# One stretch of filler products per inverse level instead of two, in a two-block transformer kernel

## The chip, the cores and the metric

The kernel runs on one core of one Trainium2 chip. The metric is the device time of one execution in microseconds, the median of several runs. TensorE does the matrix products, VectorE (DVE) and ScalarE (ACT) the elementwise work and the copies out of PSUM, GpSimd (POOL) a little elementwise work, and SyncE (SP) issues the weight transfers.

## The reference, cut to what matters

Two blocks run one after the other on a sequence of 256 tokens of width 1024, all in float32. The first has a mixer and a mixture-of-experts layer, twice. The second is this, for each of two layers, cut to the branch that the change touches:

```python
def rwkv7_scan(r, w, k, v, kk, a):
    # S_t = S_{t-1} diag(w_t) - (S_{t-1} kk_t) (kk_t * a_t)^T + v_t k_t^T ; y_t = S_t r_t
    ...

def rwkv_branch(r, k, v, wl, al, gate, w0, w_up, a0, a_up, k_k, k_a, r_k, lnx_g, lnx_b):
    ...
    y = rwkv7_scan(r_h, w_h, k_h, v_h, kk, a_h)
    mu = jnp.mean(y, axis=-1, keepdims=True)
    var = jnp.mean(jnp.square(y - mu), axis=-1, keepdims=True)
    y = ((y - mu) * lax.rsqrt(var + GN_EPS)).reshape(B, S, W_C) * lnx_g.astype(f32) + lnx_b.astype(f32)
    bonus = jnp.sum(r_h * k_h * r_k.astype(f32), axis=-1, keepdims=True) * v_h
    out = (y + bonus.reshape(B, S, W_C)) * jax.nn.silu(gate.astype(f32))
```

Around it stand the input projection `h @ w_in` (its columns hold the queries, keys and values of three branches, their gates, and three merge gates of width 1024), two attention branches, and the merge of the three.

## The kernel before, in words

**The recurrence.** The kernel does not step through the 256 tokens. It cuts them into chunks of 64 and turns each chunk into small matrices. A layer `l` has 8 heads, in two halves `p` of 4, so `recurrence(l, p)` runs four times. Its heart is the inverse of 16 triangular 64x64 matrices, by doubling: it starts from 2x2 blocks and takes five levels (`for n in range(1, LEVELS)`). A level is a closed chain of three engines:

- TensorE, `step` (L1749): 16 products of 64x64, for two head groups `hh`. Before it TensorE waits for VectorE's updates of the level before (`Sv.at("inv", *K, n - 1, hh)`) and for a mask by GpSimd (`level`).
- ScalarE (L978): one copy out of PSUM per `hh`, signal `step`.
- TensorE: `transposed` (L1762) and `forward` (L1755), 32 products of 64x64 in all (24 in the last level), each group waiting for its copy.
- VectorE (L2591): one subtraction per `hh`, signal `inv`, which starts the next level.

**The filler.** While TensorE waits for such links it takes products from a generator, `fill_tiles(l)` (L1641). Each `next(filler)` issues one dense product of 128x128 by 128x256, called a unit here. A layer has 12 jobs of 16 units (the gates of the three branches, then six tiles of merge gates), 192 units, and the assertions below `filled_by` want all 192 used by the end of `recurrence(l, 1)`. How many units stand at which point is written out by hand in `FILLS`: in "level" before the change, one between `step` and the wait for its first copy, and two behind the products, ahead of the next level. Jobs alternate between PSUM banks 7 and 6; job `n` may start when ScalarE has taken job `n - 2` out (`fill_out`). ScalarE does that at the points where `filled(point)` finds, from `FILLS`, that a job is complete. The weights of the jobs pass through a ring of four slots, and every second job's last product frees one (`used`), for which SyncE waits before it issues the next transfer.

**The norm.** Behind the recurrence's reads, TensorE makes the mean (`gn_mean`, L1892), VectorE centres (L2621), ScalarE squares (L996), TensorE sums (`gn_sum`, L1896), ScalarE makes the inverse root (L1000, L1002), and VectorE scales, adds and multiplies (L2517 to L2517), signal `o`. `fill("gn_mean")` stands between the two TensorE products, `fill("gn_sum")` behind the second. With `p` = 1 two projections of the next stage (`latent`, L1260) stand between `gn_sum` and its filler. With `p` = 0 the next `recurrence(l, 1)` follows the filler, beginning with the `lora` products (L1688); ScalarE's first work there (L949) waits for `o`.

Of the kernel before, what the change touches and what calls it, by code (L numbers as in the profile page):

```python
# [52 lines left out]
H2 = 8  # L53
FILL_POINTS = ["open", "down", "lora", "kk_sum", "rk_sum", "tok"] + ["level"] * (LEVELS - 1) + [
    "w1", "gh", "y0", "move1", "move2", "read", "gn_mean", "gn_sum"]
FILL = dict(tok=6, level=3, w1=2, gh=2, y0=2, move1=1, move2=1, read=2, gn_mean=4)
FILLS = {(0, 0): dict(FILL, open=6, down=0, lora=5, kk_sum=15, rk_sum=8, gn_sum=27),
         (1, 0): dict(FILL, open=4, down=2, lora=11, kk_sum=14, rk_sum=8, gn_sum=22),
         (0, 1): dict(FILL, open=0, down=0, lora=6, kk_sum=15, rk_sum=8, gn_sum=32)}
FILLS[1, 1] = FILLS[0, 1]  # L60
BRANCHES = (2, 0, 1)
NORM_FILL = (0, 6, 6, 10, 4, 6, 8, 8, 16, 16, 16)
# [263 lines left out]
def two_block_program(nc, w, out, cum_rows, marks, order):  # L326
# [34 lines left out]
    with ExitStack() as ctx:  # L361
# [18 lines left out]
        def bank(b, n=HALF):  # L380
            return ps_t[:, b * HALF:b * HALF + n]
# [259 lines left out]
        def filled_by(l, p, point):  # L641

            before = sum(FILLS[l, 0][x] for x in FILL_POINTS) if p else 0
            return (before + sum(FILLS[l, p][x] for x in FILL_POINTS[:point + 1])) // (2 * KD)

        for l in range(2):
            assert filled_by(l, 1, len(FILL_POINTS) - 1) == 12
            assert sum(FILLS[l, p][x] for p in range(2) for x in FILL_POINTS) == 12 * 2 * KD
        POINTS = len(NORM_FILL)
# [524 lines left out]
        def _(pe):  # L1174
# [82 lines left out]
            def project(dst, lhs, rhs, n=KD):  # L1257

                for k in range(n):
                    mm = M(dst, lhs(k), rhs(k), start=k == 0, stop=k == n - 1)  # L1260
                return mm
# [319 lines left out]
            def second(l):  # L1581
# [29 lines left out]
                filler = fill_tiles(l)  # L1611
                for _ in range(FILLS[l, 0]["open"]):
                    next(filler)
                if l:
# [4 lines left out]
                    project(bank(2, T)[0:32], lambda k: vdw[:, k], lambda k: s2["rkv"][:, 2, k], 4).then_inc(*Sp.up("v_down"))  # L1619
                    for _ in range(FILLS[l, 0]["down"]):  # L1620
                        next(filler)
# [5 lines left out]
                for p in range(2):  # L1627
                    recurrence(l, p, lora, ht, filler)
                attention_parts(l)

            def fill_tiles(l):

                for n, (key, i, _) in enumerate(fill_jobs(l)):
                    if i == 0:
                        pe.wait_ge(*has_landed(key))
                    if n >= 2:
                        pe.wait_ge(*S("fill_act").at(l, n - 2))
                    for x in range(2):
                        for k in range(KD):
                            c = (2 * i + x) * P  # L1640
                            mm = M(bank(fill_bank(n))[:, x * T:x * T + T], slot(key)[:, k, c:c + P], s2["ht"][:, k],  # L1641
                                   start=k == 0, stop=k == KD - 1)
                            if x and k == KD - 1:
                                if i:
                                    mm.then_inc(used, 1)
                                else:
                                    mm.then_inc(*S("fill_pe").up(l, n))
                            yield
# [24 lines left out]
            def recurrence(l, p, lora, ht, filler):  # L1673
                Sa, Sp, Sv, So = S("rwkv_act"), S("rwkv_pe"), S("rwkv_dve"), S("rwkv_pool")
                K = (l, p)
# [41 lines left out]
                for r, (jj, tt) in enumerate(pairs):  # L1717
                    for hh, half, o in ((0, 0, 0), (1, 1, 0), (1, 0, T)):
                        for c in range(2):
                            rows, tok = halves[hh], slice(tt * P + 64 * c, tt * P + 64 * c + 64)  # L1720
# [20 lines left out]
                inv, prod, wk, gh = rw["inv"], rw["prod"], rw["wk"], rw["gh"]  # L1741
# [4 lines left out]
                def step(n, hh, r, c):  # L1746

                    rows = halves[c]
                    return M(bank(2 + hh)[halves[(c + hh) % 2], r * 64:r * 64 + 64], rw[f"lev{n % 2}"][rows, r, hh], inv[rows, hh, 0, r],  # L1749
                             start=True, stop=True)  # L1750

                def forward(hh, r, c):

                    rows = halves[c]
                    return M(bank(hh)[halves[(c + hh) % 2], r * 64:r * 64 + 64], inv[rows, hh, 1, r], prod[rows, hh, r],  # L1755
                             start=True, stop=True)

                def transposed(hh, r, c):

                    rows = halves[c]  # L1760
                    o = (256, 3 * HALF)[hh] + r * 64
                    return M(ps_t[rows, hh * HALF + o:hh * HALF + o + 64], prod[rows, hh, r], inv[rows, hh, 1, r],  # L1762
                             start=True, stop=True)

                each = [(r, c) for r in range(4) for c in range(2)]
                for n in range(1, LEVELS):
                    pe.wait_ge(*So.at("level", *K, n))
                    for hh in range(2):
                        pe.wait_ge(*Sv.at("inv", *K, n - 1, hh))
                    for r in range(4):  # L1770
                        for hh in range(2):
                            for c in range(2):
                                mm = step(n, hh, r, c)
                            if r == 3:
                                mm.then_inc(*Sp.up("step", *K, n, hh))
                    next(filler)
                    if n == 1:
                        pe.wait_ge(*Sv.at("gk", *K))
                    pe.wait_ge(*Sa.at("step", *K, n, 0))
                    for r, c in each:  # L1780
                        mm = transposed(0, r, c)
                    pe.wait_ge(*Sa.at("step", *K, n, 1))
                    if n == LEVELS - 1:
                        mm.then_inc(*Sp.up("inv", *K, n, 0))
                        for r, c in each:
                            mm = forward(1, r, c)
                        mm.then_inc(*Sp.up("inv", *K, n, 1))
                    else:
                        for r in range(4):
                            for hh in range(2):  # L1790
                                for c in range(2):
                                    mm = forward(hh, r, c)
                                if (r, hh) == (3, 0):
                                    mm.then_inc(*Sp.up("inv", *K, n, 0))
                        for r, c in each:
                            mm = transposed(1, r, c)
                        mm.then_inc(*Sp.up("inv", *K, n, 1))
                    for _ in range(FILLS[K]["level"] - 1):
                        next(filler)

                vt, bht, kht = rw["v_tok"], rw["bh_tok"], rw["kh_tok"]
# [1202 lines left out]
```

## Time and profile before

| | |
|---|---|
| median of 3 runs | 2031.74 us (2028.92 to 2032.73) |
| profiled execution | 2032.98 us, its span 2031.2 us |
| TensorE busy | 1653.0 us, 81% of the span |
| VectorE, ScalarE, GpSimd busy | 27%, 16%, 5% |
| mean granted TensorE clock | 0.909 |

The span is cut into 40 slices of 50.8 us. The first 24 are the first block, which reads the experts' weights; the second block begins near 1222 us. In the rows below, PE is TensorE's products and PEld its weight loads. Every float32 product shows as two records of each, so a unit is two PE records, and `x4` is two units. The time behind `[` is how long the engine had been idle before the row, and behind `<-` stands what ended it. The end of a PE record is modelled and overlaps the next one, so lengths of TensorE work are best taken from start to start. A row of a stretch (A:B) has its length, then for PE, PEld, DVE, ACT and POOL the busy time with the number of records (for one line alone, PE and PEld only), then the mean granted clock (1.00 is 2.4 GHz, 0.50 is 1.2 GHz), the DMA share and GB/s. A row of waits has the total, the number of waits and the longest; `issue` means that nothing in the profile ended it.

### The profile page before, as it was taken

How to read it: one execution, taken by the hardware profiler on the slowest of the kernel's cores; microseconds unless marked ns; L12 is line 12 of the kernel's file. 1: busy time of each engine (PE TensorE's matmuls, PEld its weight loads, DVE VectorE, ACT ScalarE, POOL GpSimd, SP SyncE). 2: the span in 40 equal slices, each digit the busy share in tenths (PEclk: the TensorE clock that was granted, in tenths of full speed). 3: DMA queues.
4: the chain of work that ended last, by engine and by line, in shares of the span. 5: the costliest groups of instructions: out<-in, count | busy, mean ns of one | idle time of the engine just before them, and what ended most of it. 6: DMA issues, size and time to landing. Idle time of an engine off the chain costs nothing.

```text
span 2031.2 us, 25724 instructions
## 1 busy us (share of the span) xinstructions
PE 1653.0 (81%) x11442; PEld 946.6 (47%) x11442; DVE 543.5 (27%) x1029; ACT 335.0 (16%) x723; POOL 106.4 (5%) x129
## 2 busy tenths in 40 slices
PE   6988765666757997565656569999999999999999
PEld 3544221111215862111212118777578687775785
DVE  0455010000105652000101012553343225533432
ACT  1131100000000001000000001343332013423320
POOL 0000000000000001000000000210020002100200
PEclk8998898877888998787888779999999999999999
DMA  9988999999999969999999992321443331214330
GB/s 403 385 372 341 426 428 428 428 428 428 428 428 425 393 264 415 423 428 427 428 428 428 428 426 94 126 85 48 187 145 125 135 144 65 92 48 172 146 125 21
DMA packets 45740, 588.66 MB, mean 290 GB/s; under 512 B 5184, under 2 KB 5344, under 8 KB 9920
## 3 DMA queue, kind: packets, MB, share of 16 engines
q1 hardware_dynamic: 42624, 575.05, 68.7%
q0 software_dynamic: 2576, 10.54, 1.3%
q8 instruction: 90, 1.47, 0.3%
q10 hardware_dynamic: 432, 1.44, 0.2%
q14 instruction: 18, 0.15, 0.0%
HBM read 585.96 MB, written 1.06 MB: 289 GB/s over the span
## 4 chain that ended last, share of the span: by engine, by line
PE 56%; DMA 38%; DVE 3%; ACT 2%; issue 1%; SPq 0%; ACTq 0%; DVEq 0%
DMA arena<-in_experts 37%; PE ps L1260 17%; PE ps L1641 8%; PE ps L1528 5%; PE ps L1664 4%; PE ps L1660 4%; PE ps L1433 3%; PE ps L2015 3%; DMA ring<-in_stream 1%; PE ps L1762 1%; PE ps L2028 1%; PE ps L1749 1%; PE ps L2071 1%; PE ps L1224 1%; PE ps L1540 1%
## 5 line engine op out<-in xcount | busy, mean ns | idle before, releaser
L1528 PE MATMUL ps<-arena 128*32 128x512 f32 x1532 | 246.3, 768 | 149.3 <-DMA arena<-in_experts 144.7
L1528 PE MATMUL ps<-ring,arena 128*32 128x512 f32 x1488 | 232.6, 755 | 148.5 <-DMA ring<-in_experts 148.3
L1528 PEld LDWEIGHTS ps<-arena 128*32 128x32 f32 x1532 | 49.8, 126 | 303.0 <-DMA arena<-in_experts 150.4
L1528 PEld LDWEIGHTS ps<-ring,arena 128*32 128x32 f32 x1488 | 47.0, 124 | 304.1 <-DMA ring<-in_experts 180.6
L1641 PE MATMUL ps<-arena,ring 128*128 128x256 f32 x768 | 188.0, 388 | 0.0
L1260 PE MATMUL ps<-arena,ring 128*128 128x256 f32 (+1 forms) x960 | 184.1, 354 | 2.5 <-ACT arena L754 2.5
L1260 PEld LDWEIGHTS ps<-arena,ring 128*128 128x128 f32 x960 | 163.6, 193 | 22.7 <-ACT arena L754 3.1
L1641 PEld LDWEIGHTS ps<-arena,ring 128*128 128x128 f32 x768 | 139.8, 190 | 29.4 <-issue 10.1
L2448 DVE TENSOR_TENSOR arena<-ps,gate 128x512 f32<-128x512 f32 x16 | 10.3, 686 | 315.6 <-PE ps L1528 315.6
L1660 PE MATMUL ps<-arena,ring 128*128 128x256 f32 x384 | 89.5, 382 | 0.0
L862 ACT ACTIVATE arena<-ps,modcol 128x128 f32<-128x128 f32 x32 | 14.6, 457 | 439.0 <-PE ps L1540 439.0
L1664 PE MATMUL ps<-ring,arena 128*128 128x512 f32 x192 | 85.7, 592 | 0.0
L1260 PE MATMUL ps<-arena 128*128 128x256 f32 (+1 forms) x384 | 76.8, 365 | 4.0 <-ACT arena L1144 2.5
L2444 DVE TENSOR_TENSOR arena<-ps,arena 128x512 f32<-128x512 f32 x16 | 10.3, 686 | 257.9 <-PE ps L1528 257.9
L1660 PEld LDWEIGHTS ps<-arena,ring 128*128 128x128 f32 x384 | 70.9, 190 | 11.6 <-issue 3.0
L1260 PEld LDWEIGHTS ps<-arena 128*128 128x128 f32 x384 | 68.0, 207 | 12.6 <-ACT arena L1144 2.5
L1540 PEld LDWEIGHTS ps<-arena,h 128*128 128x128 f32 x256 | 36.7, 208 | 51.0 <-issue 49.8
L1260 PE MATMUL ps<-ring,arena 128*128 128x128 f32 (+3 forms) x192 | 55.4, 445 | 0.0
L2015 PE MATMUL ps<-ring,ln 128*128 128x512 f32 x128 | 55.3, 592 | 0.0
L868 ACT ACTIVATE arena<-ps 128x512 f32<-128x512 f32 x16 | 9.6, 597 | 271.5 <-PE ps L1564 271.5
L1664 PEld LDWEIGHTS ps<-ring,arena 128*128 128x128 f32 x192 | 35.2, 190 | 37.4 <-issue 37.3
L2430 DVE TENSOR_SCALAR arena<-ps,modcol 128x128 f32<-128x128 f32 x32 | 13.1, 409 | 134.3 <-PE ps L1540 134.3
(400 smaller groups left out, 1861.6 us busy)
## 6 DMA issues: line engine op xcount, KB each, us to landing
arena<-in_experts SPq DMA_DIRECT2D x95, 2048.0 KB, 36.0
ring<-in_experts SPq DMA_DIRECT2D x93, 2048.0 KB, 36.1
ring<-in_stream SPq DMA_DIRECT2D x61, 2048.0 KB, 8.8
arena<-in_stream SPq DMA_DIRECT2D x14, 2048.0 KB, 19.5
ring<-in_stream SPq DMA_DIRECT2D x2, 1696.0 KB, 7.2
arena<-in_stream SPq DMA_DIRECT2D x2, 1024.0 KB, 27.6
gate<-in_b_mod POOLq DMA_DIRECT2D x4, 512.0 KB, 11.2
ln<-in_experts SPq DMA_DIRECT2D x2, 1024.0 KB, 7.6
```

The lines of the kernel that those rows point to most:

```text
L1224: mm = M(bank(mod_bank((l, j)))[o:o + 32], md["condT"][:, k, 6 - 2 * at:38 - 2 * at], slot(key)[:, k], start=k < 4 and at == 0, stop=k >= ...
L1260: mm = M(dst, lhs(k), rhs(k), start=k == 0, stop=k == n - 1)
L1433: mm = M(bank(2 * a + j), mix[:, k, a * P:(a + 1) * P], slot(key)[:, k], start=i == 0, stop=i == KD - 1)
L1528: mm = M(bank(b + half)[32 * e:32 * e + 32], x[:, k, 32 * e:32 * e + 32], wk(e, half), start=k == 0, stop=k == KD - 1, tile_position=(0, 3 ...
L1540: mm = M(bank(7 - k % 2)[:, k // 2 * P:k // 2 * P + P], h[:, a, k * P:(k + 1) * P], ff["pick"][:, a, g * P:(g + 1) * P], start=a == 0, sto ...
L1641: mm = M(bank(fill_bank(n))[:, x * T:x * T + T], slot(key)[:, k, c:c + P], s2["ht"][:, k], start=k == 0, stop=k == KD - 1)
L1660: mm = M(bank(fill_bank(n))[:, x * T:x * T + T], slot(key)[:, k, c:c + P], s2["ht"][:, k], start=k == 0, stop=k == KD - 1)
L1664: mm = M(bank(fill_bank(n)), s2["ht"][:, kk, i * P:(i + 1) * P], slot(key)[:, kk], start=kk == 0, stop=kk == KD - 1)
L1749: return M(bank(2 + hh)[halves[(c + hh) % 2], r * 64:r * 64 + 64], rw[f"lev{n % 2}"][rows, r, hh], inv[rows, hh, 0, r], start=True, stop=True)
L1762: return M(ps_t[rows, hh * HALF + o:hh * HALF + o + 64], prod[rows, hh, r], inv[rows, hh, 1, r], start=True, stop=True)
L2015: mm = M(bank(2 * a + j), merged[:, k, a * P:(a + 1) * P], slot(key)[:, k], start=k == 0, stop=k == KD - 1)
L2028: return M(bank(hh)[:, a * P:a * P + n], q[rows, j, a * P:(a + 1) * P], k[rows, j, 0:n], start=True, stop=True)
```

## The change

In each of the five levels of each of the four recurrences the unit between `step` and the wait for its copy is gone; the two behind the products stay. That frees 5 units per recurrence. With `p` = 0 they are added to `gn_sum` (27 to 32 in layer 0, 22 to 27 in layer 1), with `p` = 1 to `gn_mean` (4 to 9). The number of units per layer stays 192, and ScalarE's points for taking jobs out follow from the same tables.

```diff
-FILL = dict(tok=6, level=3, w1=2, gh=2, y0=2, move1=1, move2=1, read=2, gn_mean=4)
-FILLS = {(0, 0): dict(FILL, open=6, down=0, lora=5, kk_sum=15, rk_sum=8, gn_sum=27),
-         (1, 0): dict(FILL, open=4, down=2, lora=11, kk_sum=14, rk_sum=8, gn_sum=22),
-         (0, 1): dict(FILL, open=0, down=0, lora=6, kk_sum=15, rk_sum=8, gn_sum=32)}
+FILL = dict(tok=6, level=2, w1=2, gh=2, y0=2, move1=1, move2=1, read=2, gn_mean=4)
+FILLS = {(0, 0): dict(FILL, open=6, down=0, lora=5, kk_sum=15, rk_sum=8, gn_sum=32),
+         (1, 0): dict(FILL, open=4, down=2, lora=11, kk_sum=14, rk_sum=8, gn_sum=27),
+         (0, 1): dict(FILL, open=0, down=0, lora=6, kk_sum=15, rk_sum=8, gn_sum=32, gn_mean=9)}
 FILLS[1, 1] = FILLS[0, 1]
...
                                 mm = step(n, hh, r, c)
                             if r == 3:
                                 mm.then_inc(*Sp.up("step", *K, n, hh))
-                    next(filler)
                     if n == 1:
                         pe.wait_ge(*Sv.at("gk", *K))
                     pe.wait_ge(*Sa.at("step", *K, n, 0))
...
                         mm.then_inc(*Sp.up("inv", *K, n, 1))
-                    for _ in range(FILLS[K]["level"] - 1):
+                    for _ in range(FILLS[K]["level"]):
                         next(filler)
```

## Rows read from the trace of the kernel before

**Rows 1.** The page: TensorE's row and the 40 slices.

```profile
PE   6988765666757997565656569999999999999999
PEclk8998898877888998787888779999999999999999
```

**Rows 2.** Busy time by stretch: levels of (0,0); norm of (0,1) with its projections.

```profile
1298.40:1317.20 18.80, 18.80 (x479) 14.56 (x478) 5.89 (x10) 3.89 (x11) 4.23 (x6) 1.00 0.01 3
...
1401.80:1430.60 28.80, 28.80 (x110) 20.46 (x110) 5.79 (x16) 10.46 (x27) 1.15 (x4) 1.00 0.26 92
```

**Rows 3.** Waits of TensorE's products, 1230 us to the end.

```profile
PE ps L1921 <- issue: 2.1, 2, 1.0
PE ps L1734 <- issue: 1.4, 1, 1.4
...
PE ps L1885 <- issue: 1.0, 1, 1.0
PE ps L1693 <- ACT arena L954: 0.9, 3, 0.4
PE ps L1697 <- DVE arena L2549: 0.3, 1, 0.3
```

**Rows 4.** Timeline, second level of (0,0): weight loads, copies, updates.

```profile
1302.26 0.58 PEld L1749 LDWEIGHTS ps<-arena 64*64 64x64 f32 x32 [0.33 <-issue]
1302.90 0.30 PEld L1641 LDWEIGHTS ps<-arena,ring 128*128 128x128 f32 x2
1303.00 0.66 ACT L978 ACTIVATE arena<-ps 128x256 f32<-128x256 f32 x2 [3.21 <-PE ps L1749]
1303.53 0.54 PEld L1762 LDWEIGHTS ps<-arena 64*64 64x64 f32 x16 [0.33 <-ACT arena L978]
1303.94 0.60 PEld L1755 LDWEIGHTS ps<-arena 64*64 64x64 f32 x32
1304.73 1.28 DVE L2591 TENSOR_TENSOR arena<-arena,ps 128x512 f32<-128x512 f32 x2 [2.60 <-PE ps L1755]
1305.08 0.73 PEld L1641 LDWEIGHTS ps<-arena,ring 128*128 128x128 f32 x4
1306.14 0.65 PEld L1749 LDWEIGHTS ps<-arena 64*64 64x64 f32 x32 [0.33 <-issue]
```

**Rows 5.** The copies of all levels by line: shortest, median, longest ns.

```profile
L978 ACT ACTIVATE arena<-ps x40: 378/381/384, 1299.1 to 1791.7; 128x256 f32<-128x256 f32 x40
```

**Rows 6.** Timeline: a square on ScalarE and the weight load that waited for it.

```profile
1349.30 0.65 ACT L954 ACTIVATE arena<-arena 128x512 f32<-128x512 f32 x1
...
1349.99 0.30 PEld L1693 LDWEIGHTS ps<-arena,tab 128*128 128x128 f32 x2 [0.63 <-ACT arena L954]
```

**Rows 7.** The chain that ended last, norm of (0,1) with what follows.

```profile
1402.85 1.73 PE ps L1641 x8
1404.58 0.92 PE ps L1896 x2
1405.50 11.39 PE ps L1260 x32
1416.89 13.81 PE ps L1641 x64
```

**Rows 8.** Timeline: the norm's square and scaling, ends of filler, (0,0).

```profile
1333.13 0.30 PEld L1896 LDWEIGHTS ps<-arena,tab 128*128 128x128 f32 x2 [0.20 <-ACT arena L996]
...
1334.10 11.82 PE L1641 MATMUL ps<-arena,ring 128*128 128x256 f32 x54
...
1338.00 0.69 DVE L2517 TENSOR_TENSOR arena<-arena 128x512 f32<-128x512 f32 x1
...
1345.84 1.14 PE L1688 MATMUL ps<-arena,small 64*128 64x256 f32 x8
```

**Rows 9.** Busy time by stretch: one line's products around a rise of the clock.

```profile
1225.00:1227.80 2.80, 2.80 (x14) 2.80 (x15) 0.50 0.00 0
1228.60:1231.40 2.80, 2.80 (x27) 2.80 (x27) 1.00 0.00 0
```

## The prediction

> **What bounds the kernel now.** I read the page first. Its 40 slices show two regimes: in the first block TensorE is busy 5 to 9 tenths, from slice 25 on it is at 9 throughout, with the granted clock at its upper digit [rows 1]. The change is wholly in the second block, so the question is what limits TensorE there. Two stretches answer it: in the levels of (0,0) TensorE is busy 18.80 of 18.80 us, in the norm of (0,1) with its projections and filler 28.80 of 28.80 us, both at clock 1.00 (2.4 GHz) [rows 2]. The list of waits says the same for the whole block: the waits of TensorE's products shown come to 5.7 us of some 800, the list has two more entries, shorter than the first shown, none is for a transfer, and none stands at L1762, at L1896 or behind a filler of `gn_sum` [rows 3]. So the block's time is TensorE's issue time plus a few holes. A change that leaves the number of products as it is can gain only where there is a hole to fill, or where a unit is dearer in one place than in another. That is what I look for.
>
> **What a unit costs in each place.** In a dense run, 64 records, which are 32 units, take 13.81 us: 0.2158 us per record, 0.432 us per unit [rows 7]. In a level the single unit is dearer. Its weight load starts at 1302.90 and the first load of the products behind it at 1303.53: 0.63 us [rows 4]. The load of small weights comes 0.33 us after the unit's last load ends, and the same 0.33 us stands before `step` behind two units, where 1305.08 to 1306.14 is 1.06 us for two [rows 4]. So changing from dense to small products costs about 0.20 us once per stretch (0.63 - 0.43, and 1.06 - 0.86). Taking one of two stretches out of a level takes one change-over out with it. This is the part that speaks for the change.
>
> **What waits when the unit is gone.** The products L1762 need the first copy. In the level shown, the two copies begin at 1303.00 and take 0.66 us together [rows 4]; a single one has a median of 0.381 us, and the 40 copies lie between 0.378 and 0.384 [rows 5], two in each of 20 levels. The first copy therefore ends at 1303.38. What TensorE needs after a ScalarE end, when it really stands waiting, shows at L1693: the square ends at 1349.30 + 0.65 = 1349.95, the weight load starts at 1349.99, 0.04 us later [rows 6]. So without the unit the products could start at 1303.42, against 1303.53 now. The copies themselves start no earlier, since they wait for `step`, which begins the level. The gain is 0.11 us per level. The second copy ends at 1303.66, and its products (L1755) come 0.41 us behind the first, 1303.53 to 1303.94 now [rows 4], so at 1303.83: that wait stays covered.
>
> The rest of the level moves as a block. VectorE's updates start when products are done and end at 1304.73 + 1.28 = 1306.01, TensorE's two units let `step` start at 1306.14 [rows 4]. Both ends hang on the same products, both come 0.11 us earlier, and the units still end last by about 0.1 us. GpSimd's mask (4.23 us busy in 18.80) has room [rows 2].
>
> Bounds of this term. At worst the wait takes as long as the unit did, gain 0. At best TensorE may start when ScalarE starts its second copy: two copies of 0.381 in 0.66 us put that at 1303.28, so 1303.32 with the same 0.04, gain 0.21. I take 0.11, since the row with a real wait (L1693) was released by an end. Over 20 levels: 2.2 us, between 0 and 4.2.
>
> **What the freed units cost where they go.** 20 units at 0.432 are 8.6 us. What hole do they fill?
>
> *`gn_mean` of `p` = 1, 10 units.* The four units there run from 1402.85 to 1404.58, 1.73 us, which is exactly 8 records at the dense pace, and `gn_sum` follows at once [rows 7]. In (0,0) its weight load is released by the square, 0.20 us after the load before [rows 8], but L1896 does not appear among the products' waits [rows 3]. `gn_sum` with its two records takes 0.92 us where two records of twice the columns take 4 x 0.2158 = 0.86 at the dense pace. At the most 0.06 us per norm is to be had, 0.1 us in all. I take nothing. The five units more are 2.16 us ahead of `gn_sum`. What is late then is the norm's chain behind it, but the projections (11.39 us) and the 32 units (13.81 us) stand between it and TensorE's next need for it [rows 7], and they move with it.
>
> *`gn_sum` of `p` = 0, 10 units.* The filler ends at 1345.84, when `lora` starts. VectorE's last step of the norm ends at 1338.69 [rows 8]. The norm is already covered for 7 us too long, so five units more are plain work in front of `lora`. ScalarE's take-out of the last job, its table load and the sigmoids follow the filler's end, so the 0.2 to 0.4 us wait at L1693 [rows 3] stays.
>
> *What else moves.* Taking a job out moves to another point in each recurrence, in (0,0) into the norm itself (64 units are now full at the end of `gn_mean`, not in "read"), between the square and the table load. That puts a copy of about 0.6 us, my estimate from two PSUM copies of half the size in 0.66 us [rows 4], into a chain with 7 us of room. In the levels, `(0,0)` has unit 48 end right before `step` of the fifth level, where ScalarE may start its first copy up to 0.1 us late, once. The job that frees a ring slot ends some 3 to 10 us later in two recurrences, and its successor (`latent`) is used at 1405.50 [rows 7], 70 us later. I cost all three at nothing. The last job before a shift of recurrences, 96, is complete at the same point as before.
>
> **The sum.** +8.6 for 20 units in dense places, -2.2 for 20 levels: +6.4 us. Counted the other way: 20 units at 0.63 leave (12.6), 20 waits of 0.52 (0.63 - 0.11) and 20 units at 0.432 come, which is the same. The profiled execution took 2032.98 us (span 2031.2 and 1.8 around it), so 2039.4; it lies 1.2 us above the median of 2031.74, for which I say 2038.2 us. With the bounds of the wait, +4.4 to +8.6: 2036.1 to 2040.4.
>
> **Rivals.**
>
> *The clock falls in the levels (slower still).* The levels would hold 20 standstills of half a microsecond, where the trace shows TensorE without a hole. The product rows around a rise show the price of the lower level: 14 records in 2.80 us at 0.50 against 27 in 2.80 us at 1.00, so a factor of two [rows 9]. If half of the 75 us of levels (20 x 3.8) fell to 1.2 GHz, 19 to 37 us would come. Against it: the hole of 1.0 us at L1921 and that of 1.4 us at L1734 [rows 3] stand in a block whose clock digit never leaves 9 [rows 1]. The Trainium skill, TensorE: Matmul & The Clock Gate, section "A second HAM failure mode: psum-queue depth-cycling", tells of a kernel in which short idle times between groups of products made the clock swing; by that rule this change would lose tens of microseconds. The trace does not bear it out for holes of a microsecond or more. Chance 0.03.
>
> *The wait is dearer than a row shows (slower).* If release and restart of small products cost 0.1 us more than at L1693, the level gains nothing: +8.6 us, 2040.4. Chance 0.12.
>
> *Holes that nothing explains move (no change).* Four waits of L1921, L1734 and L1885 with no releaser make 4.5 us [rows 3]. Their place may hang on the order of instructions. If all four went, +1.9 us is left, 2033.6; two of them, or copies that release early (gain 0.21), bring it to about +4. They may as well grow. Chance 0.19 for within 4 us.
>
> *The copies do not gate the level (faster).* If the level gives back the unit's whole 0.63 us, the change brings 20 x (0.432 - 0.63) = -4.0 us, 2027.7. It decides from 0.43 us per level on. But the first copy begins 0.74 us after `step` does, and the products would then have to start 0.10 us before it began; the modelled records could hide some of that, not 0.3 us of it. Chance 0.05, and 0.02 for anything else of that sign.
>
> **From these to the numbers.** A measurement of this kernel can tell about 0.2%, 4.1 us, from no change. The likeliest case, +4.4 to +8.6, has 0.59. Slower by over 0.2% has 0.59 + 0.12 + 0.03 = 0.74; within 0.2% has 0.19; faster 0.07. The range leaves 0.1 out on either side: from 2033.6, the case without the four holes, to 2042.5, the dear wait with 2 us for the spread of the runs (they spread over 3.8 us).
>
> **What would show it.** Right: from L1749's first record of a level to the next level's, 3.77 us in place of 3.88; L1762 listed with waits of about 0.5 us for ScalarE's L978, some 10 us in 20 waits; 64 records of filler behind `gn_sum` of (0,0) at 0.216 each, `lora` still right behind; 18 records between L1892 and L1896 at `p` = 1; clock 1.00. Wrong: a period below 3.45 us, a clock under 1.00 in the levels, or new waits at L1688 or L1641.

## The result: 0.33% slower, and the profile after

The changed kernel takes 2037.1 us (median of 7, 2033.45 to 2040.25), the kernel before 2030.72 (median of 7, 2028.15 to 2033.06). The ratio is 1.0033, interval 1.0023 to 1.0043, which is +4.7 to +8.7 us. The medians lie 6.4 us apart, the sum of the prediction; the profiled execution took 2034.81 us (span 2033.0).

The levels show both halves of the sum. First the timeline of the second level of (0,0), cut to weight loads, copies and updates, which answers to [rows 4] (lines up to L1775 keep their numbers, those behind are one lower):

```profile
1300.47 0.57 PEld L1749 LDWEIGHTS ps<-arena 64*64 64x64 f32 x32 [0.33 <-issue]
1301.20 0.66 ACT L978 ACTIVATE arena<-ps 128x256 f32<-128x256 f32 x2 [3.21 <-PE ps L1749]
1301.63 0.54 PEld L1762 LDWEIGHTS ps<-arena 64*64 64x64 f32 x16 [0.60 <-ACT arena L978]
1302.04 0.60 PEld L1755 LDWEIGHTS ps<-arena 64*64 64x64 f32 x32
1302.83 1.29 DVE L2590 TENSOR_TENSOR arena<-arena,ps 128x512 f32<-128x512 f32 x2 [2.50 <-PE ps L1755]
1303.18 0.73 PEld L1641 LDWEIGHTS ps<-arena,ring 128*128 128x128 f32 x4
1304.24 0.58 PEld L1749 LDWEIGHTS ps<-arena 64*64 64x64 f32 x32 [0.33 <-issue]
```

The first product loads its weights 1.16 us after `step` does, against 1.27 before, and the period is 3.77 us, against 3.88. A unit of 0.43 us went and 0.11 us came back. That holds in levels 2 to 5. Level 1 gave nothing back. The first products of levels 1 and 2 of (0,0), before and then after:

```profile
1298.40 0.69 PE L1749 MATMUL ps<-arena 64*64 64x64 f32 x32
1302.28 0.69 PE L1749 MATMUL ps<-arena 64*64 64x64 f32 x32
```

```profile
1296.61 0.70 PE L1749 MATMUL ps<-arena 64*64 64x64 f32 x32
1300.48 0.69 PE L1749 MATMUL ps<-arena 64*64 64x64 f32 x32
```

The period is 3.88 us before and 3.87 after, and it is 3.87 or 3.88 after the change in all four recurrences. e6 below shows why. The waits of TensorE's products from 1230 us on, against [rows 3]:

```profile
PE ps L1762 <- ACT arena L978: 9.6, 20, 0.6
PE ps L1920 <- issue: 2.1, 2, 1.0
PE ps L1260 <- ACT arena L754: 1.3, 1, 1.3
PE ps L1693 <- ACT arena L954: 0.9, 3, 0.4
PE ps L2056 <- DVE arena L2779: 0.8, 2, 0.4
PE ps L1697 <- DVE arena L2548: 0.3, 1, 0.3
```

There are 20 new waits, one per level, 9.6 us, and no other new kind. Where the freed units arrived, the chain that ended last shows dense runs, against [rows 7] (rows of (0,0), then of (0,1)):

```profile
1329.34 1.73 PE ps L1641 x8
1331.07 0.92 PE ps L1895 x2
1331.99 13.83 PE ps L1641 x64
...
1402.33 3.88 PE ps L1641 x18
1406.22 0.86 PE ps L1895 x2
1407.08 11.39 PE ps L1260 x32
```

18 records in 3.88 us and 64 in 13.83 us are 0.216 us each, as before. `gn_sum` is shorter with p = 1 alone, 0.86 for 0.92 us in (0,1) and in (1,1): that 0.06 us each is all that was uncovered. The clock is 1.00 in the levels although TensorE is now busy only 17.03 of 19.43 us there (stretch from the first `step` of (0,0) through its `w1`):

```profile
1296.67:1316.10 19.43, 17.03 (x502) 14.05 (x501) 5.89 (x10) 3.89 (x11) 4.24 (x6) 1.00 0.01 3
```

**One profile against another.** From the first projection of the second block (the `L1260 x48` row, 1224.80 before, 1222.98 after) to the end, the two profiled executions took 806.4 and 810.0 us, only 3.6 apart. The difference to 6.4 is mostly in the holes without a releaser: 4.5 us before, 2.1 us after. Without them the block took 801.9 and 807.9. The table below uses this number, and the experiments come back to the holes. The number has a spread of its own: a second profile of the kernel before (e7) gives 802.4, so half a microsecond says nothing. Most of that lies ahead of the levels. From the first `step` of (0,0) to the end, again without the holes, both profiles of the kernel before give 728.3 us, and the kernel after gives 734.3.

### The profile page after: what moved, and what is told of

It reads as the page before. It is cut to its first block, busy times and chain, and to the rows that moved or that the text cites. A ratio compares the mean times of both kernels' runs of the same rounds, so it can differ in the third digit from the quotient of the medians.

```text
span 2033.0 us, 25724 instructions
## 1 busy us (share of the span) xinstructions
PE 1645.6 (81%) x11442; PEld 945.5 (47%) x11442; DVE 542.7 (27%) x1029; ACT 335.0 (16%) x723; POOL 106.7 (5%) x129
## 3 DMA queue, kind: packets, MB, share of 16 engines
HBM read 585.96 MB, written 1.06 MB: 289 GB/s over the span
## 4 chain that ended last, share of the span: by engine, by line
PE 55%; DMA 39%; DVE 3%; ACT 2%; issue 1%; SPq 0%; ACTq 0%; DVEq 0%
DMA arena<-in_experts 37%; PE ps L1260 17%; PE ps L1641 8%; PE ps L1528 5%; PE ps L1664 4%; PE ps L1660 4%; PE ps L1433 3%; PE ps L2014 3%; DMA ring<-in_stream 1%; PE ps L1762 1%; PE ps L2027 1%; PE ps L2070 1%; PE ps L1749 1%; PE ps L1224 1%; PE ps L1540 1%
## 5 line engine op out<-in xcount | busy, mean ns | idle before, releaser
L1528 PE MATMUL ps<-ring,arena 128*32 128x512 f32 x1488 | 239.2, 774 | 151.4 <-DMA ring<-in_experts 151.4
L1528 PE MATMUL ps<-arena 128*32 128x512 f32 x1532 | 239.1, 747 | 146.1 <-DMA arena<-in_experts 141.6
L1260 PE MATMUL ps<-arena,ring 128*128 128x256 f32 (+1 forms) x960 | 184.1, 354 | 2.5 <-ACT arena L754 2.5
L1641 PE MATMUL ps<-arena,ring 128*128 128x256 f32 x768 | 182.6, 386 | 0.0
L1260 PEld LDWEIGHTS ps<-arena,ring 128*128 128x128 f32 x960 | 163.7, 193 | 22.7 <-ACT arena L754 3.1
L1660 PE MATMUL ps<-arena,ring 128*128 128x256 f32 x384 | 89.5, 382 | 0.0
L1260 PE MATMUL ps<-arena 128*128 128x256 f32 (+1 forms) x384 | 75.2, 359 | 4.0 <-ACT arena L1144 2.5
L1260 PEld LDWEIGHTS ps<-arena 128*128 128x128 f32 x384 | 66.5, 201 | 12.6 <-ACT arena L1144 2.5
L1260 PE MATMUL ps<-ring,arena 128*128 128x128 f32 (+3 forms) x192 | 55.4, 445 | 0.0
```

Of the source, the lines that this page charges most:

```text
L1528: mm = M(bank(b + half)[32 * e:32 * e + 32], x[:, k, 32 * e:32 * e + 32], wk(e, half), start=k == 0, stop=k == KD - 1, tile_position=(0, 3 ...
```

## The experiments

All times are medians; the ratio is to the kernel before on the same chip. "Block" is the second block of the profiled execution without its holes, as just worked out (span, less the start of the first projection, less the `issue` rows of the waits).

| kernel | us | before, us | ratio (interval) | block, us |
|---|---|---|---|---|
| before | | | | 801.9 |
| after | 2037.1 | 2030.72 | 1.0033 (1.0023 to 1.0043) | 807.9 |
| e1, middle unit moved behind | 2037.97 | 2031.61 | 1.0040 (1.0026 to 1.0054) | 808.6 |
| e2, only gn_mean grows | 2032.64 | 2031.61 | 1.0005 (0.9996 to 1.0014) | 802.4 |
| e3, one unit behind goes | 2037.19 | 2031.61 | 1.0026 (1.0015 to 1.0038) | 808.7 |
| e4, no unit in the levels | 2050.07 | 2031.61 | 1.0097 (1.0082 to 1.0113) | 820.5 |
| e5, p = 0 only | 2033.7 | 2031.26 | 1.0015 (1.0007 to 1.0024) | 805.8 |
| e6, gk wait ahead (one run) | 2038.94 | | | 808.2 |
| e7, before again (one run) | 2032.02 | | | 802.4 |
| e8, w1 in the levels | 2030.37 | 2031.26 | 0.9997 (0.9987 to 1.0007) | 802.5 |
| e9, and its copy early | 2029.99 | 2031.82 | 0.9987 (0.9979 to 0.9996) | 800.2 |
| e10, and three units behind lora | 2026.75 | 2031.82 | 0.9979 (0.9969 to 0.9988) | 798.7 |

### e1: the loss is in the middle, not in the norm

```diff
-                    next(filler)
                     if n == 1:
...
-                    for _ in range(FILLS[K]["level"] - 1):
+                    for _ in range(FILLS[K]["level"]):
```

> In each level the middle unit moves behind the products (0 in the middle, 3 behind); nothing goes to the norm. Theory (a bare wait of 0.52 us is left in the middle, and a unit costs 0.43 us dense wherever it goes): the level grows from 3.88 to 3.77 + 0.43 = 4.20 us, in all +6.4 us, the same as the change. Rival (the change loses where the units arrive, in the norm): no loss from the middle, so 0 to -2 us here. The clock rival: a granted clock under 1.00 in the levels.

It came out at +6.4 us by the medians (1.0040, 1.0026 to 1.0054). The chain of (0,0), level 2 up to level 3 (the shortest rows left out):

```profile
1301.30 0.64 PE ps L1749 x32
1301.96 0.39 ACT arena L978
1302.40 0.62 PE ps L1762 x14
1303.02 0.05 PE ps L1755
1303.08 0.47 PE ps L1755 x30
1303.54 0.47 PE ps L1762 x16
1304.01 1.49 PE ps L1641 x6
1305.50 0.64 PE ps L1749 x32
```

The period is 4.20 us, as forecast (4.29 in level 1, where again nothing came back), and three units behind the products take 1.49, which is two (1.06) and a dense one (0.43). With nothing moved to the norm the loss is the whole of the change's. The norm as the place of the loss is out.

### e2: the place behind gn_mean costs nothing and gives nothing

```diff
-         (0, 1): dict(FILL, open=0, down=0, lora=6, kk_sum=15, rk_sum=8, gn_sum=32)}
+         (0, 1): dict(FILL, open=0, down=0, lora=6, kk_sum=15, rk_sum=8, gn_sum=27, gn_mean=9)}
```

> The levels stay as before; with p = 1 five units move from behind gn_sum to between gn_mean and gn_sum (9 and 27). Theory (the place behind gn_mean was already covered, so a unit costs the same there as behind gn_sum): 0 us, within 0.3. Rival (delaying the norm's chain costs): +1 us or more, up to 2 x 2.2 = +4.3 us, with a new wait behind the projections. Rival (the norm's wait had a hole): -0.5 us or more.

The ratio is 1.0005, and 1 lies in its interval (0.9996 to 1.0014); the block is that of the kernel before in its second profile (802.4). The norm's chain is 2.2 us later, and nothing waits for it.

### e3 and e4: what the units behind the products cover

```diff
-FILL = dict(tok=6, level=3, w1=2, ...
+FILL = dict(tok=6, level=2, w1=2, ...
```

(e3, with the other edits to `FILLS` of the change; the line in the middle stays. e4 has `level=0`, no line in the middle, `range(FILLS[K]["level"])`, `gn_sum` 42 and 37 for p = 0 and `gn_mean` 19 for p = 1.)

> The middle unit stays, one of the two behind the products goes, and the freed units go where the change puts them. Theory (behind the products the level waits for VectorE's second update, which ends 0.13 us before the two units do): levels 1 to 4 shrink by only about 0.08 us each, level 5 by the unit's 0.43 since nothing waits there; 20 units come back at 0.43. In all 16 x 0.35 = +5.6 us, with TensorE waiting about 0.35 us at L1749 for L2591. Rival (only the middle place is special): 0 us, as a unit dearer by nothing behind the products.

> No unit in any level; 15 units per recurrence go to gn_sum (p = 0) or gn_mean (p = 1). Theory: +6.4 us for the middle ones; behind the products, levels 1 to 4 shrink from 3.77 to 3.70 us, 16 x (0.86 - 0.08) = +12.5 us; behind level 5 a whole stretch with its change-over goes, 4 x (0.86 - 1.06) = -0.8 us. In all +18.1 us (ratio 1.009), and a level's period of 3.70 us. If the clock falls because of the holes (rival): much more than 25 us, with a granted clock under 1.00 in the levels.

e3 lost 5.6 us by the medians (+3.0 to +7.7 by the interval), e4 18.5 us (+16.7 to +23.0). The intervals contain the forecasts, 5.6 and 18.1, but the forecast periods were off, both by some 0.08 us. Products and updates of e3, then of e4 (cut):

```profile
1303.60 0.59 PEld L1749 LDWEIGHTS ps<-arena 64*64 64x64 f32 x32 [0.75 <-issue]
1303.63 0.69 PE L1749 MATMUL ps<-arena 64*64 64x64 f32 x32 [0.38 <-DVE arena L2591]
1306.08 1.28 DVE L2591 TENSOR_TENSOR arena<-arena,ps 128x512 f32<-128x512 f32 x2 [2.60 <-PE ps L1755]
1307.52 0.40 PE L1749 MATMUL ps<-arena 64*64 64x64 f32 x11 [0.38 <-DVE arena L2591]
```

```profile
1299.86 0.69 PE L1749 MATMUL ps<-arena 64*64 64x64 f32 x32 [1.00 <-DVE arena L2590]
1302.21 1.28 DVE L2590 TENSOR_TENSOR arena<-arena,ps 128x512 f32<-128x512 f32 x2 [2.50 <-PE ps L1755]
1303.64 0.35 PE L1749 MATMUL ps<-arena 64*64 64x64 f32 x9 [1.01 <-DVE arena L2590]
```

e3's period is 3.89 us, that of before but for 0.01, and e4's 3.78, that of after. One unit or none behind the products makes none of levels 1 to 4 shorter: from the update's end (1307.36) to `step` (1307.52) pass 0.16 us, so two units of 1.06 just meet the chain. There they are free. The middle unit is nearly so: it lengthens levels 2 to 5 by 0.11 us and does 0.43 us of work. Behind level 5 nothing waits, and a unit costs what it costs elsewhere. From the first `step` to `w1`, the products behind level 5, a recurrence takes 18.75 us in e7's profile of the kernel before and 18.31 in e3.

With these lengths the sum for e3 is 20 x 0.432 - 4 x 0.44 = +6.9 us, and its block is 6.8 longer. That the medians say 5.6, exactly the forecast, is luck: the forecast counted on 16 levels that shrink by 0.08. For e4 (16.97 us from `step` to `w1`) the same sum is 60 x 0.432 - 4 x 1.78 = +18.8, and the block is 18.6 longer.

e4 also answers the rival of the falling clock. TensorE stands for half a microsecond in every level and for a whole one between levels, is busy 12.88 of 19.00 us, and the clock stays at 1.00, here and in the other three recurrences:

```profile
1297.00:1316.00 19.00, 12.88 (x468) 11.48 (x470) 5.89 (x10) 3.60 (x11) 4.05 (x6) 1.00 0.02 3
```

### e5: half the change, half the loss

```diff
-                    next(filler)
+                    if p:
+                        next(filler)
```

(with `level=2` and the larger `gn_sum` for p = 0 only)

> The change for p = 0 alone: its levels lose the middle unit, gn_sum gets 5 more; p = 1 is as before. Theory (each level loses 0.32 us wherever its unit goes): half of the change, 10 x 0.32 = +3.2 us. Rival (one of the two destinations carries the loss): near 0, or near the whole 6.4.

1.0015 (1.0007 to 1.0024) is +1.4 to +4.9 us, with the expected 3.2 in the middle, and the block is 3.9 us longer. Neither half carries the loss alone.

### e6: a satisfied wait in front of the real one

```diff
+                pe.wait_ge(*Sv.at("gk", *K))
                 for n in range(1, LEVELS):
...
-                    if n == 1:
-                        pe.wait_ge(*Sv.at("gk", *K))
                     pe.wait_ge(*Sa.at("step", *K, n, 0))
```

> The changed kernel with the wait for gk, long satisfied, moved from between step and the products of level 1 to ahead of the levels. In the changed kernel L1762 starts 0.14 us after the first copy's end in level 1, where that second wait stands, and 0.04 in levels 2 to 5. Theory (a second wait in a row costs the restart 0.1 us though it is satisfied): 0.04 us in level 1 too. Rival (level 1 is late for another reason, a mask or an update): 0.14 stays. The time: at most 0.4 us less, not to be seen in one run.

The changed kernel, level 1 (first copy and first product), then the same of e6:

```profile
1297.34 0.66 ACT L978 ACTIVATE arena<-ps 128x256 f32<-128x256 f32 x2 [2.62 <-PE ps L1749]
...
1297.86 0.62 PE L1762 MATMUL ps<-arena 64*64 64x64 f32 x14 [0.56 <-ACT arena L978]
```

```profile
1299.90 0.66 ACT L978 ACTIVATE arena<-ps 128x256 f32<-128x256 f32 x2 [2.62 <-PE ps L1749]
...
1300.33 0.62 PE L1762 MATMUL ps<-arena 64*64 64x64 f32 x14 [0.47 <-ACT arena L978]
```

From the copy's start to the product are 0.52 us in the changed kernel and 0.43 here, as in levels 2 to 5. The wait for `gk` had been met 2.1 us before the copy ended (VectorE made `gk` by 1295.58), and yet it cost 0.09 us. It did so in all four recurrences: the period of level 1 is 3.79 or 3.80 us in e6, and the waits at L1762 come to 9.2 us in 20 against 9.6. `step` stands behind three waits (the mask and two updates), which would fit its 0.14 to 0.16 us in e3; but that restart is released by VectorE and not by ScalarE, and it was not taken apart.

### e7: the holes fall partly by chance

> The kernel before once more, for its profile. Theory (the holes of about 1 us with no releaser belong to the program, to its order of instructions): at L1921 twice, L1734 and L1885 once, 1.0 to 1.4 us each, as in the first profile. Rival (they fall anywhere, by chance): other lines or another number.

The waits of its second profile, cut:

```profile
PE ps L1921 <- issue: 2.1, 2, 1.0
PE ps L2057 <- DVE arena L2780: 1.4, 2, 0.9
PE ps L1260 <- ACT arena L754: 1.3, 1, 1.3
PE ps L1885 <- issue: 1.0, 1, 1.0
```

The hole of 1.4 us at L1734 is not there; the same program had it in its first profile. Those at L1921 are in all twelve profiles (under the line's shifted numbers), those at L1734 and L1885 come and go. The expectation was wrong for that one hole. What the holes are stays open. They explain why one pair of profiles differs by less than the medians, and not what the change costs.

### e8 to e10: other work for the middle

e1 to e4 say what a middle is worth: 0.52 us from the end of `step` to the products that need its copy. A dense unit there pays for a change-over. The 16 small products `w1`, which need nothing of the inverse, should not. The core of e8's edit (the old place of `w1` behind the levels and the filler there go too):

```diff
+                    if n == 2:
+                        pe.wait_ge(*Sa.at("tok", *K, 3))
+                        w1(0, 1)
+                    elif n == 3:
+                        w1(2, 3).then_inc(*Sp.up("w1", *K))
+                    else:
+                        next(filler)
```

In this kernel `w1` shares columns of PSUM bank 4 with `transposed` of the second head group, so part of `w1` is lost to it; the instructions and their order are those meant.

> The kernel before, but the 16 small w1 products stand half in the middle of level 2 and half in the middle of level 3, in place of the unit there; the filler behind w1 goes, and the 4 freed units per recurrence go to gn_sum (p = 0) or gn_mean (p = 1). Theory (the middle is a wait of 0.52 us that anything may fill, small products without the change-over of 0.20 us): two middles 2 x (0.54 - 0.63), the w1 stretch -1.08 and its filler -1.06, four dense units +1.73, so -0.59 us per recurrence, -2.4 us in all (ratio 0.9988). Rival (w1 was hidden where it stood, or gh now waits for the last update): 0 or more.

The ratio is 0.9997 (0.9987 to 1.0007). In (0,0) it worked: from the first `step` to `gh` 18.66 us (1298.55 to 1317.21), where before took 20.96 (1298.40 to 1319.36), 2.30 less for 1.73 of units moved. Level 2 with half of `w1` in its middle is 3.79 us long, no longer than with the bare wait (3.78). With p = 1 a new wait came, here in (1,1):

```profile
1791.31 1.13 PE L1641 MATMUL ps<-arena,ring 128*128 128x256 f32 x4
1792.47 0.60 ACT L928 ACTIVATE arena<-ps 128x512 f32<-128x512 f32 x1 [1.95 <-PE ps L1641]
1792.97 0.59 ACT L982 ACTIVATE arena<-ps 128x512 f32<-128x512 f32 x1
1793.61 1.96 PE L1823 MATMUL ps<-arena 64*64 64x128 f32 x32 [1.17 <-ACT arena L982]
```

ScalarE's program has the take-out of a job (L928) ahead of the copy of `w1` (L982). With two units fewer by then (levels 2 and 3), that job ends with level 5's last unit, ScalarE waits for it, and `gh` waits for the copy behind it: 1.17 us, 2.3 in two recurrences. e9 puts the copy right behind those of level 3 and the result into bank 5:

```diff
+                    if n == 3:
+                        act.wait_ge(*Sp.at("w1", *K))
+                        A(rw["wk"][:, :, :, 0:64], bank(5).rearrange(...), ACT.Copy).then_inc(*Sa.up("w1", *K))
                     filled(5 + n)
```

> As the kernel with w1 in the middle of levels 2 and 3, but the result goes to PSUM bank 5 and ScalarE copies it right behind the copies of level 3, no longer behind the take-out of a job that ends with level 5. In that kernel's trace the two recurrences with p = 1 waited 1.2 us each for the late copy, which ate the gain. Theory: the wait is gone, -0.59 us per recurrence, -2.4 us against before (ratio 0.9988). Rival (the gain is lost for another reason, too): 0.

0.9987 (0.9979 to 0.9996) is -2.6 us (-0.8 to -4.3), the medians lie 1.8 apart, and the wait is gone. The interval excludes no change, narrowly. e10 adds `lora=12` in (1,0) and `lora=7` for p = 1, one unit each from `gn_sum` and `gn_mean`:

> The kernel before this one in the list, and one unit more behind lora in the three recurrences whose trace shows a wait at L1693 (0.9 us in three), taken from gn_sum or gn_mean. Theory (filler pays where there is a hole without cover): the three waits go, -0.9 us more, -3.3 us against before (ratio 0.9984); the unit is 0.43 us and the holes 0.2 to 0.4, so the chain behind moves by what is over. Rival (the hole is only moved on to L1697): -2.4 us as without it.

0.9979 (0.9969 to 0.9988) is -4.3 us (-2.4 to -6.3); the medians, 2026.75 and 2031.82 us, lie 5.1 apart. The waits of e10 from 1228 us on:

```profile
PE ps L1931 <- issue: 2.1, 2, 1.0
PE ps L1261 <- ACT arena L754: 1.3, 1, 1.3
PE ps L2067 <- DVE arena L2790: 1.0, 2, 0.6
PE ps L1642 <- ACT arena L930: 0.4, 1, 0.4
PE ps L1698 <- DVE arena L2559: 0.3, 1, 0.3
```

The wait for the square (L1693, here L1694) is gone, none came at L1698 beyond the 0.3 that was there, and a unit now waits 0.4 us once for a job's take-out. The block is 1.5 us shorter than e9's, for 0.9 expected; the other 0.6 is the wait at L2067, 1.6 us in e9 and 1.0 here, which differs between two profiles of one program as well (1.1 and 1.4 at L2057 in the kernel before). The intervals of e9 and e10 overlap, so what the three units alone bring is shown by the traces and not by the times. e10 beats both kernels.

## Why the prediction was right

- **What bounds the block.** TensorE's issue time. Right: the loss follows the units wherever they go (e1, e2, e5).
- **A unit: 0.43 us dense, 0.63 in the middle.** Right, 0.216 us per record in 64 and in 18.
- **The wait: first product at +1.16, 0.11 us gained per level.** Right in levels 2 to 5. In level 1 the gain was nothing, since the satisfied wait for `gk` cost 0.09 us. The step took its 0.04 us from L1693, a place with one wait only. So the rival of the dearer wait ("0.1 us more than at L1693, the level gains nothing") came true in four of the 20 levels. From the first `step` to `w1` the recurrences take 18.34 us after the change, against 18.75 in e7's profile of the kernel before (18.82 in two recurrences of its first profile, each with one level of 3.95 or 3.96 us that e7 does not have). That is 0.41 us gained, four times 0.10, and 1.6 us in all where the sum has 2.2.
- **The sum, +6.4 us.** With 1.6 us for the levels and 0.1 for `gn_sum` it would be +6.9. The medians give 6.4, the interval 4.7 to 8.7, the blocks 6.0: the mechanism is right, and the agreement to a tenth is luck.
- **"The units still end last by about 0.1 us".** Mis-sized: they end level with the update, since the restart there, behind three waits, takes 0.14 to 0.16 us, not 0.04. It did not matter to the change, for both ends moved alike. It mattered to e3 and e4, whose periods came out at 3.88 to 3.89 and 3.78 us instead of 3.80 and 3.70.
- **Where the units go: no hole.** Right. With p = 1 it was 0.06 us at `gn_sum`, as bounded, and e2 shows the rest as nothing. With p = 0 the units run at the dense pace, and no new wait stands behind them.
- **What else moves.** The take-out in the norm of (0,0) and the later transfers cost nothing visible: no wait of TensorE names them. e8 shows that the caution was due: there the same shift of a take-out cost 1.2 us.
- **Rivals.** The clock did not fall: it stayed at 1.00 in the levels of the changed kernel and of e4, with TensorE busy 17.03 of 19.43 and 12.88 of 19.00 us. By the Trainium skill, TensorE: Matmul & The Clock Gate, section "A second HAM failure mode: psum-queue depth-cycling", short standstills between groups of products made the clock swing; here they did not, with 0.46 and 1.0 us in each level of 3.78. The dearer wait came true in level 1 alone. Copies that do not gate are excluded by the 20 new waits for L978. The moving holes were real, and took 2.4 us off the first pair of profiles, but by chance and not by the change.

## What to carry to other kernels

Ask of every filler what it adds to the chain where it stands, not how long it is: here 0.43 us of work added 0.11 us in the middle of a level and none behind the products of levels 1 to 4, so taking it out lost 0.32 and 0.43 us. Where a chain is already covered for 7 us, more cover buys nothing. A short hole between small products takes small products of the same shape without the 0.20 us of a change-over (level 2 of e8), and when units move, look at what else a helper engine does at the point where a job now ends.

## What the runs showed of the hardware

- A wait that had been met for 2.1 us, in front of the real one, delayed TensorE's restart: 0.52 us from the copy's start with two waits, 0.43 with one (the changed kernel and e6).
- A change from dense 128x128 to 64x64 products cost 0.20 us (0.63 us for one unit in the middle of a level, 0.43 in a dense run).
- Standstills of 0.46 and 1.0 us in each 3.78 us of 64x64 products left the granted clock at 1.00 (e4).
- TensorE stood for 0.9 to 1.7 us with no releaser at two to four places of the second block; some came and went between profiles of the same program (e7).
